# Sixteen bias table transfers move from the scalar engine's queue to the sync engine's

## The reference, cut to what matters

```python
for i in range(DEPTH):                      # DEPTH = 2
    h = rms_norm(x, ffn1_norm[i])
    x = x + 0.5 * swiglu(h, ffn1_w_gate[i], ffn1_w_up[i], ffn1_w_down[i])
    h = rms_norm(x, mix_norm[i])
    x = x + (even_mixer if i % 2 == 0 else odd_mixer)(h, ..., rel_bias)
    h = rms_norm(x, ffn2_norm[i])
    x = x + 0.5 * swiglu(h, ffn2_w_gate[i], ffn2_w_up[i], ffn2_w_down[i])
# swiglu(x) = (silu(x @ w_gate) * (x @ w_up)) @ w_down, inner width 2816
# attention: logits + rel_bias[rel_bucket(t - s)], one bias per head and distance
```

## Time and profile before

| | us |
|---|---|
| median of 3 runs | 1921.73 |
| lowest and highest of the runs | 1921.44, 1924.72 |
| span of the profiled execution, first to last instruction | 1922.5 |
| PE busy | 1887.3 (98%) |
| DVE busy | 1462.5 (76%) |
| ACT busy | 1020.9 (53%) |

### The profile page before, as it was taken

One profiled execution on the slowest core, in us unless ns is written; L12 is line 12 of the kernel. 1 busy time (PEld: TensorE's weight loads), 2 busy tenths in 40 slices (PEclk: granted clock), 3 DMA queues, 4 the chain that ended last, 5 costly groups with the idle time before them and its releaser, 6 DMA issues.

```text
span 1922.5 us, 31441 instructions
## 1 busy us (share of the span) xinstructions
PE 1887.3 (98%) x11902; PEld 1674.8 (87%) x11902; DVE 1462.5 (76%) x2330; ACT 1020.9 (53%) x1640; POOL 193.0 (10%) x251
## 2 busy tenths in 40 slices
PE   7999999999999999999999999999999999999999
PEld 6899799888878899898889989887778779898997
DVE  8878487667779778597887949756988878687684
ACT  7546154477776455264644626454455766364451
POOL 1311010000001111010110101011111001011010
PEclk9999999999999999999999999999999999999999
DMA  7666862321126655462466646166765376566441
GB/s 240 169 171 182 131 188 61 110 77 57 65 102 173 170 151 152 149 175 97 136 167 165 166 132 181 50 152 161 171 148 133 85 202 171 157 168 168 133 115 66
DMA packets 94662, 271.18 MB, mean 141 GB/s; under 512 B 10568, under 2 KB 10824, under 8 KB 94512
## 3 DMA queue, kind: packets, MB, share of 16 engines
q1 hardware_dynamic: 63456, 201.22, 31.7%
q0 software_dynamic: 29232, 64.50, 19.4%
q10 hardware_dynamic: 1824, 3.44, 1.0%
HBM read 223.07 MB, written 2.28 MB: 117 GB/s over the span
## 4 chain that ended last, share of the span: by engine, by line
PE 85%; DVE 8%; ACT 3%; issue 2%; DMA 1%; ACTq 0%; DVEq 0%
PE ps_unit L797 12%; PE ps_unit L798 12%; PE ps_unit L799 12%; PE ps_y L861 6%; PE ps_y L863 6%; PE ps_y L862 6%; PE ps_s L861 4%; PE ps_s L863 4%; PE ps_s L862 4%; PE ps_t L861 4%; PE ps_t L863 3%; PE ps_t L862 3%; PE ps_s L797 1%; PE ps_s L798 1%; PE ps_s L799 1%
## 5 line engine op out<-in xcount | busy, mean ns | idle before, releaser
L1398 ACT ACTIVATE gw_hi<-gu 128x512 fp32r<-128x512 f32 (+1 forms) x400 | 318.9, 799 | 151.0 <-PE ps_s L863 67.5
L1932 DVE TENSOR_TENSOR gw_lo<-gu,gw_hi 128x512 fp32r<-128x512 f32 (+1 forms) x400 | 354.8, 901 | 49.0 <-ACT gw_hi L1398 36.7
L797 PE MATMUL ps_unit<-a_hi,w_hi 128*128 128x512 f32 x892 | 352.8, 395 | 9.2 <-DVE w_lo L1860 6.5
L798 PE MATMUL ps_unit<-a_lo,w_hi 128*128 128x512 f32 x892 | 349.1, 391 | 0.0
L799 PE MATMUL ps_unit<-a_hi,w_lo 128*128 128x512 f32 x845 | 330.1, 391 | 0.0
L1333 ACT ACTIVATE w_hi<-raw 128x1024 fp32r<-128x1024 f32 (+1 forms) x125 | 125.2, 1003 | 314.0 <-PE ps_unit L799 296.3
L797 PEld LDWEIGHTS ps_unit<-a_hi,w_hi 128*128 128x128 f32 x892 | 168.4, 189 | 48.8 <-DVE w_lo L1860 9.4
L2065 DVE TENSOR_TENSOR t<-ps_unit,half 128x512 f32<-128x512 f32 x96 | 66.4, 691 | 172.4 <-PE ps_unit L799 171.8
L798 PEld LDWEIGHTS ps_unit<-a_lo,w_hi 128*128 128x128 f32 x892 | 168.4, 189 | 33.2
L799 PEld LDWEIGHTS ps_unit<-a_hi,w_lo 128*128 128x128 f32 x845 | 159.5, 189 | 34.1
L861 PE MATMUL ps_y<-xu_hi,gw_hi 128*128 128x256 f32 x640 | 180.3, 282 | 0.3 <-ACT sqb L1402 0.3
(11 more groups left out here) (322 smaller groups left out, 4666.9 us busy)
## 6 DMA issues: line engine op xcount, KB each, us to landing
gu<-gu_stream_dram SPq DMA_DIRECT2D x176, 512.0 KB, 5.2
raw<-w_stream_dram SPq DMA_DIRECT2D x136, 512.0 KB, 3.3
gu<-gu_stream_dram SPq DMA_DIRECT2D x80, 256.0 KB, 3.0
gu<-gu_stream_dram POOLq DMA_DIRECT2D x80, 256.0 KB, 4.5
gu<-gu POOLq DMA_DIRECT2D x80, 256.0 KB, 3.3
w_lo<-raw POOLq DMA_DIRECT2D x28, 512.0 KB, 5.1
raw<-w_stream_dram SPq DMA_DIRECT2D x32, 384.0 KB, 3.5
w_lo_3rd<-raw POOLq DMA_DIRECT2D x15, 512.0 KB, 5.2
```

The source lines that it names most:

```text
L797: pe.matmul(ps, lhs_hi, rhs_hi, start=first, stop=False)
L798: pe.matmul(ps, lhs_hi, rhs_lo, start=False, stop=False)
L1398: act.activation(gw_hi[:, w, :], src, ACT.Copy).then_inc(gw_hi_done, 1)
L1932: dve.tensor_tensor(gw_lo[:, w, :], src, gw_hi[:, w, :].bitcast(F32), ALU.subtract).then_inc(gw_lo_done, 1)
```

## The change

ACT's `prepare` becomes `skew_table`, which keeps only the first step (the table's copy and the transfer to `skew`, at the end of the first group). The 16 transfers go to SP: a new `bias_load(p)` has the same access patterns. In SP's loop over the first phase's tiles, for j from 14 to 21 (`BIAS_AFTER`, the third group), two are issued after `gu_to(f + 2)`; at j = 14 SP first waits for `skewed`. The wait of VectorE for all 16 stays as it is.

```diff
--- before.py
+++ after.py
@@ -49,6 +49,7 @@
              *[(1, TE_TAPS[1] + k) for k in range(2, VE_TAPS[1])], *[(j, TE_TAPS[j] + k) for j in (2, 3) for k in range(1, VE_TAPS[j])]]
 SKEW = 640
 COPIES = 8
+BIAS_AFTER = range(GROUP_AT[2], FT)
 
 FFN_UNITS = len(GROUPS) * KT
 PAIRS = KT // 2
@@ -601,6 +602,11 @@
             def x_load(d):
                 sp.dma_start(xt_tile(d), xt_in[d]).then_inc(x_landed[d], 16)
 
+            def bias_load(p):
+
+                sp.dma_start(bias_t[p:p + COPIES, :, :], skew.rearrange("h p y -> h (p y)")[:, P - 1 - p:P - 1 - p + COPIES * (SKEW - 1)].rearrange(
+                    "h (p y) -> p h y", y=SKEW - 1)[:, :, 0:T]).then_inc(bias_landed, 16)
+
             after_mixer = [FFN_BASE[i] + r for i in range(1, len(PHASES)) if PHASES[i] == "ffn" and PHASES[i - 1] != "ffn" for r in range(2)]
             def odd_used(n):
 
@@ -664,6 +670,12 @@
                 for j in range(FT):
                     f = FFN_BASE[i] + j
                     gu_loaded = gu_to(f + 2)
+                    if i == 0 and j in BIAS_AFTER:
+                        if j == BIAS_AFTER[0]:
+                            sp.wait_ge(skewed, 16)
+                        rows = P // len(BIAS_AFTER)
+                        for p in range((j - BIAS_AFTER[0]) * rows, (j - BIAS_AFTER[0] + 1) * rows, COPIES):
+                            bias_load(p)
                     if j == 4:
                         for n in range(units_loaded, UNIT_BASE[i] + 6):
                             unit_load(n)
@@ -1484,8 +1496,8 @@
                     if more:
                         gw_high(f + 1, 4)
                     hidden_hi(f, j, i)
-                    if i == 0:
-                        prepare(g)
+                    if i == 0 and g == 0:
+                        skew_table()
                     for d in range(KT):
                         n = UNIT_BASE[i] + g * KT + d + 2
                         if n < NUNITS:
@@ -1650,18 +1662,12 @@
                 if u == 3:
                     lru_root(3)
 
-            def prepare(step):
-
-                if step == 0:
-                    act.wait_ge(table_mm, 1)
-                    act.activation(table[:, 0:T], ps_misc[0:HEADS, :], ACT.Copy).then_inc(table_done, 1)
-                    act.wait_ge(table_done, 1)
-                    act.dma_start(skew, table.rearrange("h (o y) -> h o y", o=1).to_broadcast([HEADS, COPIES + 1, SKEW])).then_inc(skewed, 16)
-                if step == 1:
-                    act.wait_ge(skewed, 16)
-                    for p in range(0, P, COPIES):
-                        act.dma_start(bias_t[p:p + COPIES, :, :], skew.rearrange("h p y -> h (p y)")[:, P - 1 - p:P - 1 - p + COPIES * (SKEW - 1)].rearrange(
-                            "h (p y) -> p h y", y=SKEW - 1)[:, :, 0:T]).then_inc(bias_landed, 16)
+            def skew_table():
+
+                act.wait_ge(table_mm, 1)
+                act.activation(table[:, 0:T], ps_misc[0:HEADS, :], ACT.Copy).then_inc(table_done, 1)
+                act.wait_ge(table_done, 1)
+                act.dma_start(skew, table.rearrange("h (o y) -> h o y", o=1).to_broadcast([HEADS, COPIES + 1, SKEW])).then_inc(skewed, 16)
 
             def mix_out(i, a):
                 n = out_base(i)
```

## The result

| | before | after |
|---|---|---|
| median, us (12 runs each, same chip) | 1922.03 | 1925.36 |
| lowest to highest, us | 1920.38 to 1924.72 | 1922.69 to 1928.80 |
| span of the profiled execution, us | 1922.5 | 1925.7 |

The changed kernel is slower by 3.3 us: ratio 1.0017, 95% interval 1.0009 to 1.0024. The prediction was 1914.5 us, in a range that ended at 1917.9. The median of the kernel before was 1921.73 in its three earlier runs and is 1922.03 here.

What follows compares the result with a forecast made beforehand. PE, busy 98% of the span, was taken as the bound, held up by the bias issues on ACT. From the median 1921.73 us, a gain of 7.2 with all other parts at zero gave 1914.5 us; range 1913.5 to 1917.9.

Steps and rivals of the forecast that it cites:

- Removed from ACT: Second group's end: 16 issues leave ACT; PE gains 6.97 us by one measure, 7.32 by another; 7.2 taken.
- Added to SP: Third group: 16 issues, 0.7 us per tile, fit where SP has some 4 us with nothing to do; cost nothing.
- Moved in time: The 2.1 MB travel from about 247 instead of 196; the mixer's first bias read, about 397, waits for nothing.
- The unknown: what eight pairs cost the loads they travel with: Third group's loads beside the pairs: zero taken, at worst 1.9 us of PE stall, growing to about 3.4 us.
- The prediction's own signs of being wrong: ACT's late-group waits before gw_hi end on DMA, PE stands still between 280 and 320, or the mixer's bias read waits.
- The cover: Tile 21's loads: landed at 298.8, read by ACT at 302.50, so 3.7 us of lateness costs nothing.
- The start: Third group: only pairs of tiles 15 to 18 delay a load; the first falls into the quiet before 254.58.
- The end: Third group's end: the last three pairs have no load behind them in a full interval.
- The first: Pairs make loads of tiles 20 and 21 late beyond cover: 0.5 to 3.4 us back, 1915.0 to 1917.9; chance 0.20.
- the second: Last six transfers delay tile 21's summed block about 3, up to 8 us: 1917.9 to 1923; chance 0.06.
- The third: Ring order: every load behind a pair waits for the whole pair, 32.8 us back, 1947; chance 0.04.
- A rate: Bias transfers alone move 35.2 packets per us, so the last six take 12.3 us.

Runs made afterwards that it cites:

- the spread: Kernel before with its 16 issues kept on ACT, three behind each w_hi of units 10 to 14 and one behind unit 15's: 1916.67 us, ratio 0.9969.
- the halved block: Kernel before with COPIES = 16, so 8 issues instead of 16 on ACT at the old place: 1916.76 us, ratio 0.9968.
- the four kernels without a stall: Issues spread on ACT 1916.67 us; 8 issues at the old place 1916.76; all on SP after tile 21's sums, 8 partitions 1916.46, 16 partitions 1915.83.
- the quiet kernel: Changed kernel with all 16 transfers issued by SP after tile 21's sum within SBUF has landed, 8 partitions each: 1916.46 us, ratio 0.9966.
- the widened kernel with the burst of three: Changed kernel with COPIES = 16: one 16-partition transfer per tile, three at once at the end: 1918.62 us, ratio 0.9978.
- the two quiet kernels: Changed kernel with all transfers issued by SP after tile 21's sums: 8 partitions each 1916.46 us, 16 partitions each 1915.83 us.

## Why the prediction was wrong, point by point

- **"Removed from ACT"**, 6.97 to 7.32 us: right, in mechanism and size. The trace after has 7.32 us, and the spread and the halved block confirm the cause without moving anything to SP. Two smaller reservations. The prediction set the span, 1922.5, against the median, 1921.73; but a run's time stands 1.8 us above its span (1927.54 against 1925.7 after), so the profiled execution was one of some 1924.3, above the median and not near it. By medians the four kernels without a stall gain 5.4 to 6.5 us; their intervals take in 7.2 (ratio 0.9963) all the same.
- **"Added to SP"**, nothing: right. The pairs took 0.67 to 0.76 us in gaps, SP's next load after the pair of 248.03 went out at 251.87, long after it, and 7.06 us of issues in one piece cost nothing in the quiet.
- **"Moved in time"**: right. VectorE's first read of the bias came at 408.4 and waited for no transfer.
- **"The unknown: what eight pairs cost the loads they travel with", bounds 0 to 3.4 us, "I take zero"**: this is the step that failed. It measured 11.57 us in the profiled execution, and some 10 by the medians (3.3 lost in all, where the quiet kernel gains 6.5). The prediction's own signs of being wrong came true with it: ACT's waits before `gw_hi` end on transfers, and PE stands still between 280 and 320. It had pieces that the runs bear out, narrow transfers that take about half of the engines' time and more work than fits beside the loads, and went wrong in three places.
  - *The cover.* It was computed from the landing of the 512 KB loads to ACT's piece 0 at 302.50: 3.7 us (with a landing of 4.7 us from another stretch; tile 21's later load took 5.5). But the loads have an earlier reader, POOL's sum within SBUF, which goes out as soon as both have landed and whose own landing ACT's piece 2 needs. That is a chain of two landings, and both were late. The other chain is like it: SP's 256 KB piece, POOL's sum from DRAM, then piece 0. In the kernel before, tile 17's sum within SBUF landed 3.6 us after 260.09, at 263.69, and ACT read it at 270.20: So this chain had a cover of 6.5 us, more than the prediction's 3.7. After, the loads made it 4.3 us late and the sum, with 8.05 us instead of 3.6, another 4.4: 8.7 us, of which the cover leaves 2.2, and ACT's wait at 265.06 is 2.19. The prediction had 5.6 us at worst after four tiles; the first tile alone had 8.7. What fails is the sum of the delays along a chain, which a bound for the largest load does not show.
  - *The start.* Only loads behind a pair were counted, "only the pairs of tiles 15 to 18", and "the first falls into the quiet before 254.58". But tile 17's second large load, issued at 247.56, just ahead of the pair of 248.03, was already 4.3 us late, and the first wait of PE came at 266.53.
  - *The end.* "The last three have none behind" was said of SP's loads. Behind them was POOL's sum of tile 21, which took 15.42 us.
- **Rivals.** The first (group 3 pays a little, 0.5 to 3.4 us) and the second (the last six starve tile 21, about 3 and up to 8 us) were offered as alternatives at 0.20 and 0.06; they came together, at some 4.5 and 6.6 us in the trace, and the measured 1925.36 us lies above the upper end of both (1923). The second named the mechanism of the burst, and its grounds against, "needs only a share of the engines", did not hold: the sum took 15.42 us. The third had the right sign and the wrong cause: with a queue of its own the bias cost as much or more.
- **A rate.** The 35.2 packets per us come from a window whose first 0.6 us hold none, so they are a little low for it; the quiet kernel, with 839 in 25 us, has 33.6, and bears the figure out.

The Trainium skill (DMA: Bandwidth & Descriptors, Rules for kernel authors, "Use all 16 engines") says that a transfer whose slowest dimension is shorter than 16 is confined to at most that many engines, and to put a multiple of 16 outermost. The runs agree: 53.5% of the engines' time with 8 partitions alone, 87.4% with 16. (The share adds up the time of all packets, also of those that overlap, and so can pass the part of the engines in use: in the widened kernel with the burst of three it is 1.13 from 290 to 300 us.)

**Left open.** Why the widened kernel with the burst of three scatters over 8 us between runs, and the half microsecond of the 11.57 that no row explains. That the pairs cost what they cost by their shape is shown by the change of the shape alone. That they do it by way of the half of the engines is an argument from the shares of the two quiet kernels: beside the loads the two queues together take 91.8% of the engines' time in the changed kernel and 97.6% in the widened one, which has no steady wait, so the total does not tell them apart, and no view here shows the engines one by one.

## What to carry to other kernels

Taking issues off a busy engine is only half of such a move: ask where the transfers themselves will then run, on which engines, and which chains of landings run there: where one transfer is issued only when another has landed, add up the delays of both and set the sum against the slack at the end of the chain. Before moving a transfer, see whether its shape uses all the engines and whether the old place has gaps: here three issues behind each split, or half as many issues of twice the size, gave all that the move was to give. And find the stretch where no loads run: the same narrow transfers cost nothing there.

## What the runs showed of the hardware that was not expected

- The same 2.1 MB in runs of 2 KB took some 34 us with 8 partitions per transfer and less than 20 with 16, at 53.5% and 87.4% of the engines' time.
- Beside the narrow transfers the large loads on the same queue did not land later in the median (4.4 us against 5.0), though single ones took 8.9 and 9.4, while POOL's 256 KB transfers took 8.1 and 9.5 us instead of 3.3 and 3.9. With the bias on a queue of its own the large loads took 8.4. So the queue shifts which loads are held up, and a queue of its own made the kernel no faster.
- `raw` loads that landed in 11.7 us in the median (the spread kernel, 190 to 250 us) instead of 3.4 (the quiet one) ended no wait of ACT, so a landing three times as long was covered there.
